# Slot weights and token placement leave PSUM in one ScalarE copy, and two ScalarE steps change places, in the expert loop of a hybrid decoder trunk

## The reference

```
y = 0
for e in range(32):
    gate, up = split(z @ w_gate_up[e])          # 1024 -> 2 x 512
    y += combine[:, e] * ((silu(gate) * up) @ w_down[e])   # 512 -> 1024
x = x + y;  out = rms_norm(x)
```

## Time and profile before

| | |
|---|---|
| median of 3 runs | 927.54 us (927.2 to 927.8) |
| the profiled execution, own time | 929.3 us |
| the profiled execution, span | 927.5 us |
| busy share of the span | TensorE 94% (weight loads 81%), VectorE 88%, ScalarE 67%, GpSimd 1% |
| mean granted TensorE clock | 0.987 of full |
| HBM traffic | 270.64 MB, 292 GB/s over the span; about 400 GB/s in the expert stage |
| chain that ended last | TensorE 48%, VectorE 30%, "issue" 14%, ScalarE 6% |

### The profile page before, as it was taken

How to read it: one execution, slowest core, us unless ns; L and a number is a source line. 1 busy time by engine, 2 the same in 40 slices (tenths; PEclk the granted TensorE clock), 3 DMA queues, 4 the chain that set the end, 5 groups by cost and what they waited for, 6 DMA issues and landing times.

```text
span 927.5 us, 14508 instructions
## 1 busy us (share of the span) xinstructions
PE 873.3 (94%) x5734; PEld 751.2 (81%) x5734; DVE 814.4 (88%) x818; ACT 621.7 (67%) x537; POOL 11.0 (1%) x19
## 2 busy tenths in 40 slices
PE   5999999999999899868999999999999999999975
PEld 5999999999899899657877777777777877777764
DVE  5358999999867957488999999999999999999993
ACT  5563434345453573558888878888888878887882
POOL 0110000000000000020000000000000000000000
PEclk9999999999999999979999999999999999999997
DMA  9952545455443486518999999999999999999911
GB/s 379 374 183 97 210 155 194 170 184 194 159 155 119 182 317 267 211 37 327 384 400 399 411 395 407 398 411 400 401 408 408 396 400 406 409 398 396 423 66 45
DMA packets 20146, 270.64 MB, mean 292 GB/s; under 512 B 2192, under 2 KB 2448, under 8 KB 3856
## 3 DMA queue, kind: packets, MB, share of 16 engines
q1 hardware_dynamic: 19696, 268.59, 73.0%
q10 hardware_dynamic: 416, 1.57, 0.5%
HBM read 269.10 MB, written 1.05 MB: 291 GB/s over the span
## 4 chain that ended last, share of the span: by engine, by line
PE 48%; DVE 30%; issue 14%; ACT 6%; DMA 1%; DVEq 1%; SPq 0%; ACTq 0%
DVE lo L932 10%; PE ps L1317 10%; PE ps L1146 9%; PE ps L1147 9%; PE ps L1148 9%; DVE lo_last L932 7%; ACT hi L578 5%; PE ps L1305 3%; DVE lo L704 2%; DVE conv L791 2%; PE ps L1161 2%; PE ps L1163 2%; PE ps L1162 2%; DVE y_lo L1055 1%; DVE hT L1041 1%
## 5 line engine op out<-in xcount | busy, mean ns | idle before, releaser
L932 DVE TENSOR_TENSOR lo<-raw,hi 128x2048 fp32r<-128x2048 f32 x142 | 323.5, 2287 | 7.6 <-ACT hi L578 6.6
L578 ACT ACTIVATE hi<-raw 128x2048 fp32r<-128x2048 f32 x141 | 264.2, 1909 | 3.5 <-PE ps L1317 3.5
L1317 PE MATMUL ps<-hi,xeT 128*128 128x512 f32 x384 | 158.4, 412 | 15.1 <-DVE lo L932 11.2
L704 DVE TENSOR_TENSOR lo<-raw,hi 128x2048 fp32r<-128x2048 f32 x62 | 141.7, 2288 | 30.0 <-ACT hi L396 28.5
L1146 PE MATMUL ps<-inA,hi 128*128 128x256 f32 x576 | 165.1, 287 | 1.6 <-DVE lo L704 1.1
L1147 PE MATMUL ps<-inA,hi 128*128 128x256 f32 x576 | 163.8, 284 | 0.0
L1148 PE MATMUL ps<-inA,lo 128*128 128x256 f32 x576 | 163.7, 284 | 0.0
L396 ACT ACTIVATE hi<-raw 128x2048 fp32r<-128x2048 f32 x63 | 120.6, 1914 | 63.6 <-PE ps L1148 41.0
L1317 PE MATMUL ps<-lo,xeT 128*128 128x512 f32 x384 | 150.7, 392 | 0.0
L1146 PEld LDWEIGHTS ps<-inA,hi 128*128 128x128 f32 x576 | 111.4, 193 | 2.7 <-DVE lo L704 2.6
L1147 PEld LDWEIGHTS ps<-inA,hi 128*128 128x128 f32 x576 | 111.5, 194 | 0.1
(11 more groups left out here) (214 smaller groups left out, 1229.5 us busy)
## 6 DMA issues: line engine op xcount, KB each, us to landing
raw<-in_w_experts SPq DMA_DIRECT2D x96, 2048.0 KB, 9.8
raw<-in_w_dense SPq DMA_DIRECT2D x29, 2048.0 KB, 7.8
raw<-in_w_dense SPq DMA_DIRECT2D x2, 1024.0 KB, 8.1
x_sb<-in_x SPq DMA_DIRECT2D x1, 1024.0 KB, 4.8
mem_sb<-in_mem SPq DMA_DIRECT2D x1, 1024.0 KB, 15.5
x_again<-in_x ACTq DMA_DIRECT2D x1, 1024.0 KB, 5.0
out<-x SPq DMA_DIRECT2D x2, 512.0 KB, 2.7
ffn_row<-in_rows ACTq DMA_DIRECT2D x1, 512.0 KB, 7.4
```

Of the source, the lines that this page charges most:

```text
L578: nc.scalar.activation(expert_half(hi, N0), raw_flat(slot, k % 2), ACT.Copy).then_inc(hi_made, 1)
L704: nc.vector.tensor_tensor(conv_half(lo, N), raw_half(slot, h), conv_half(hi, N).bitcast(f32), ALU.subtract).then_inc(lo_made, 1)
L932: nc.vector.tensor_tensor(expert_half(lo, N0), raw_flat(expert_slot(m), k % 2), expert_half(hi, N0).bitcast(f32), ALU.subtract).then_inc(l ...
L1317: last = mm(dst, xeT[:, par, 4 * (k % 2) + kt, k // 2 % 2, :], expert_half(w, N)[:, kt * 512:(kt + 1) * 512], start=(k % 4 == 0 and kt == ...
```

## The change

It does five things. The picks' two results are laid side by side in G0 (8 columns of weights, then 256 of put), and one ScalarE copy brings both to a new tile `put_parts` in SBUF; `put` is a view of it. VectorE's `slot_weights` reads the weights there, and waits for that copy (`put_made`) instead of `slotted`. ScalarE's wait for `comb_slot_made` moves from the put copy down to the up copy, which uses it. In steps 1 to 15 ScalarE converts half 6 ahead of the gate's copy instead of behind it; step 0 keeps the order. ScalarE makes the high part of y before that of h, each behind its own wait. `fold2` moves to another address.

```diff
--- before.py
+++ after.py
@@ -142,9 +142,10 @@
 
         S0 = B0 + 32 * KB
         pick2 = at("pick2", S0, [2, TT, 3 * SLOTS], bf16)
-        put = at("put", A0 + 12 * KB, [2, T], r32)
         ident_bf = at("ident_bf", S0 + 2 * KB, [P], bf16)
-        fold2 = at("fold2", S0 + 2 * KB + 512, [2, SLOTS])
+        fold2 = at("fold2", S0 + 2 * KB + 256, [2, SLOTS])
+        put_parts = at("put_parts", S0 + 2 * KB + 768, [2, 8 + T], r32)
+        put = put_parts[:, :, 8:8 + T]
 
         part = at("part", S0, [2, T])
         square_out = at("square_out", S0, [512])
@@ -630,25 +631,27 @@
                 if start:
                     more(4, 5)
                 else:
-                    more(2, 3, 4, 5)
+                    more(2, 3, 4, 5, 6)
                 act.wait_ge(half_used, used + 4)
                 if not start:
                     act.wait_ge(gate_folded, i)
                 nc.scalar.activation(gu_sb[:, 0:FF], G0, ACT.Copy).then_inc(gate_out, 1)
-                more(6, 7)
+                if start:
+                    more(6)
+                more(7)
                 if start:
                     act.wait_ge(comb_made, 1)
                     act.wait_ge(loops_made, 1)
                 expert_xeT(i + 1, (r + 1) % 2)
                 more(8)
 
-                act.wait_ge(comb_slot_made, i + 1)
                 act.wait_ge(slotted, i + 1)
-                nc.scalar.activation(put[:, r, :], G0[:, T:2 * T], ACT.Copy).then_inc(put_made, 1)
+                nc.scalar.activation(put_parts[:, r, :], G0[:, 0:8 + T], ACT.Copy).then_inc(put_made, 1)
                 more(9)
                 if not start:
                     more(10)
                 act.wait_ge(half_used, used + 8)
+                act.wait_ge(comb_slot_made, i + 1)
                 if not start:
                     act.wait_ge(up_folded, i)
                 nc.scalar.activation(gu_sb[:, FF:2 * FF], G1, ACT.Copy, scale=comb_slot[:, r:r + 1]).then_inc(up_out, 1)
@@ -660,10 +663,8 @@
                 nc.scalar.activation(silu_sb[:, :, :, :].rearrange("p f x s -> p (f x s)"), G0, ACT.Silu).then_inc(silu_made, 1)
                 if not start:
                     more(12, 13)
-                    act.wait_ge(half_used, used + 12)
+                    y_out(i - 1, used + 12)
                 hT_hi(i)
-                if not start:
-                    y_out(i - 1, used + 12)
 
             step(0, 0)
             step(0, 1)
@@ -1043,8 +1044,8 @@
 
             def slot_weights(i, par):
 
-                dve.wait_ge(slotted, i + 1)
-                parts = G0[:, 0:8].rearrange("p (x k) -> p x k", x=2)
+                dve.wait_ge(put_made, i + 1)
+                parts = put_parts[:, par, 0:8].bitcast(f32).rearrange("p (x k) -> p x k", x=2)
                 nc.vector.tensor_tensor(fold2[:, :, :],
                                         fold.rearrange("p (o s) -> p o s", o=1).to_broadcast([P, 2, SLOTS]),
                                         parts[:, :, 3:4].to_broadcast([P, 2, SLOTS]), ALU.mult).then_inc(fold2_made, 1)
@@ -1384,7 +1385,7 @@
                            start=(t == 0 and x == 0), stop=(t == TT - 1 and x == 1), skip_group_check=True)
                 for t in range(TT):
                     for x in range(2):
-                        last = mm(G0[:, T + t * P:T + (t + 1) * P], picked(t, x), ident_bf[:, :],
+                        last = mm(G0[:, 8 + t * P:8 + (t + 1) * P], picked(t, x), ident_bf[:, :],
                                   start=(x == 0), stop=(x == 1), skip_group_check=True)
                 last.then_inc(slotted, 1)
                 gate_or_up(j, at_half, 6, r)
```

## The result

| | before | after |
|---|---|---|
| median of 5 runs | 927.2 us (926.2 to 927.8) | 918.6 us (917.6 to 921.8) |
| ratio of the runs | | 0.9913, 95% interval 0.9893 to 0.9933 |
| profiled execution, span | 927.5 us | 917.5 us |
| mean granted TensorE clock | 0.987 | 0.989 |

The changed kernel is faster by 8.6 us between the medians. Lines of the changed kernel are one higher than before (578 is 579, 932 is 933), and two or three higher from the put copy to silu (647 is 649, 654 is 657).

What follows compares the result with a forecast made beforehand. VectorE was taken as the bound, with one hole per step; closing it gives 8 x 0.31 + 7 x 0.40 = 5.3 us, other terms nothing, so 927.5 becomes 922.2 us. Range: 919.9 to 925.2.

Steps and rivals of the forecast that it cites:

- The bound: In the expert stage VectorE sets the pace; its only hole is one wait per step, 3.5 us in 13 waits.
- Half 6: ScalarE converts half 6 ahead of the gate's copy, closing VectorE's 0.31 or 0.40 us hole in steps 1 to 15: 5.3 us.
- One copy for weights and put: At the put copy, ScalarE's saved 1.45 us wait is worth nothing; VectorE's new wait has 0.43 us of margin.
- the first hole: VectorE's gap before half 6's low part, whose high part ScalarE made late: 0.40 us lost, 0.31 shown as idle.
- My sign of a wrong forecast: A new VectorE wait of over 0.2 us a step anywhere, or ScalarE waiting for a transfer, would show the forecast wrong.
- Fold and reduction from SBUF: VectorE's fold and reduction read SBUF instead of PSUM: likeliest gain 0, between 2.1 us gain and 1.4 us loss.
- rival (a): SBUF sources are cheaper for VectorE's fold and reduction, 0.13 us a step, 2.1 us in all: 920.1 us; chance 12%.
- y ahead of h: ScalarE makes y's high part before h's: worth nothing, with at least 0.48 us spare before VectorE wants h's.
- all that was shifted: Loads come earlier with VectorE, 13 us of cover remain; TensorE's 0.56 us idle in a step exceeds what is taken away.

Runs made afterwards that it cites:

- The put part: Kernel before, with one copy for weights and put, VectorE reading SBUF, and ScalarE's reduction wait moved down, without the two ScalarE swaps: 924.16 us, ratio 0.9975.
- the move of half 9: Kernel before, with only ScalarE's conversion of half 9 moved ahead of the put copy and its wait for the reduction: 924.19 us, ratio 0.9976.
- the kernel with the late put copy: Changed kernel, with half 9 converted ahead of the put copy: 936.72 us, ratio 1.011.
- the kernel with `fold2` moved too: Changed kernel, with h's low part and also the product that makes fold2 done on GpSimd instead of VectorE: 907.03 us, ratio to before 0.9787.

## Why the prediction was wrong

**The bound** was right: VectorE sets the pace, and its idle time is what there was to win.

**Half 6**, 5.3 us, was right: 5.43 between the folds. The whole run agrees loosely, with 3.9 between the medians and 5.0 by the ratio.

**One copy for weights and put** is the step that failed: the prediction put the removed wait at nothing. It says: "The saved 1.45 us is ScalarE's, and ScalarE is not the bound: worth nothing", and of VectorE: "Everything else on VectorE follows back to back." Both were wrong by the same 0.15 us a step. The put copy began after VectorE's reduction, and half 9 0.28 us behind it; VectorE then made low part 8, 2.20 us of work, and wanted half 9 at 733.54, when ScalarE had it at 733.64. Since VectorE had released the copy itself, being earlier would not have helped it: the two ran a round that was 0.15 us longer than VectorE's own work. The put part and the move of half 9 show 2.1 to 2.2 us for it in 15 steps. The evidence stood in rows I had chosen: 4.49 for one pair of low parts, 4.64 for the other. I used the first to price the overlap and did not compare it with the second. The best check would have been a sum from start to start: twelve low parts at 2.20, the gathered tokens' low part at 1.14, fold and reduction at 0.27, the pick matrix at 0.47, the product at 0.60, h's low part at 0.60 and y's at 1.20 make 30.68, while I took 30.85 for VectorE's work with the first hole closed. My sign of a wrong forecast, a new VectorE wait of over 0.2 us a step, could not catch this; only the distance of the folds, 30.69 against 30.85, did.

This step explains most of the miss and not all of it. The medians put the changed kernel 3.6 us below the forecast. The 15 steps account for 2.4 of them (7.70 won against 5.3), and 0.3 is the kernel before, at 927.2 in these runs where I started from 927.54. The remaining 0.9 us is open; single executions of the changed kernel lie between 917.6 and 921.8. With the second hole in it the forecast would have been 919.8, still 0.1 below my range.

**Fold and reduction from SBUF**: 0 was right. They cost 0.20 and 0.07 us as before. The Trainium skill (Perfetto Trace Analysis, Optimizing Scalar/DVE Operations) gives VectorE about 60 ns of overhead on SBUF and 125 on PSUM; the trace shows no such difference in this kernel. By luck rival (a), with 2.1 us on top of the 5.3, gave a time of 920.1, the nearest of all to the true one, for a wrong reason.

**y ahead of h, and all that was shifted**: nothing, as said. No wait for a transfer appeared. The put copy ends at 722.75 + 0.39 = 723.14, 0.46 us before the fold; 0.43 was forecast.

**The chances**: with 0.89 on faster the sign was well placed. The range failed because it had no room for a second hole: its lower end rested on a price for SBUF alone, and no rival said that the removed wait was worth something.

## What to carry to other kernels

When one engine sets the pace, add up its own instructions from start to start over one period and compare with the period; the difference is what can be won as long as that engine goes on setting the pace, and it includes holes too short to be listed as idle. A row that merges two equal instructions and is longer than its neighbours is such a hole. A wait of an engine with time to spare costs nothing only if what is queued behind it isn't the next thing that the pacing engine needs.

## What the runs showed of the hardware that I had not expected

**TensorE's clock and single waits.** In the kernel with the late put copy, step 1 is 26.22 us long, 3.5 more than in the changed kernel, where the others lose 0.99. TensorE had stood idle for 2.66 us there, and its clock was at the lower level behind it (0.57 of full on average over 8 us). TensorE's timeline, then the busy time of the stretch behind the idle time:

```profile
435.39 0.79 PE L1318 MATMUL ps<-hi,xeT 128*128 128x512 f32 x1 [2.66 <-DVE lo L933]
```

```profile
434.00:442.00 8.00, 6.61 (x16) 5.01 (x16) 8.00 (x5) 6.32 (x4) 0.00 (x0) 0.57 0.71 261
```

In the changed kernel the idle time at this place is 1.61 us and the clock stays at 1.00. At the lower level the block of half 2 took 3.58 us (435.39 to 438.97; the changed kernel starts the next block 2.20 us after this one), and the gather, the picks and the copy behind them came late.

**GpSimd beside VectorE.** GpSimd's instruction for h's low part lasts 2.14 to 2.19 us in steps 1 to 15, and it cost VectorE 0.60. VectorE keeps its distances beside it: the low part is followed after 2.20 us and the two instructions of y's low part after 1.20, as in the earlier trace rows. GpSimd's rows in step 0 and in a later step, then VectorE's timeline across the start of the second:

```profile
430.03 1.29 POOL L384 TENSOR_TENSOR hT<-silu_sb,hT 128x512 fp32r<-128x512 f32 x1 [23.14 <-ACT hT L632]
...
700.40 2.14 POOL L384 TENSOR_TENSOR hT<-silu_sb,hT 128x512 fp32r<-128x512 f32 x1 [27.93 <-ACT hT L632]
```

```profile
699.10 2.29 DVE L948 TENSOR_TENSOR lo<-raw,hi 128x2048 fp32r<-128x2048 f32 x1
701.30 1.28 DVE L1065 TENSOR_TENSOR y_lo<-ps,y_hi 128x512 fp32r<-128x512 f32 x2
702.50 2.28 DVE L948 TENSOR_TENSOR lo<-raw,hi 128x2048 fp32r<-128x2048 f32 x1
```

The Trainium skill (Perfetto Trace Analysis, Optimizing Scalar/DVE Operations) says that GpSimd and VectorE share a read port at SBUF, so that moving work between them might not help. In this kernel it helped in full: 0.60 us a step.

The 2.1 to 2.2 us are not what GpSimd needs for this work. In step 0 no VectorE instruction runs beside it, and it takes 1.29 us. In every later step it starts while VectorE works on a low part, whose two operands lie in SBUF, and ends 1.22 to 1.26 us after that low part has made way for y's, which has one operand in PSUM (here it ends at 702.54, and y's begins at 701.30). In the kernel with `fold2` moved too it starts about 0.2 us later within the low part, lasts 1.94 to 1.99 us, and ends at the same distance (1.23 to 1.27). The trace's times on GpSimd are rough, but this pattern is the same in all 15 steps of both kernels. So it looks as if GpSimd waits for the low part to end and then works beside y's, and it is done when VectorE comes to its next low part (702.50). No run tests what happens when it starts elsewhere in the list, so the full gain is shown for this place only.

**Durations drift, distances don't.** In the profiled execution of the changed kernel VectorE's low parts last 2.32 us on average, against 2.29 in the earlier trace rows, and yet follow each other every 2.20. Only distances from start to start could be compared between executions.
